# A two-layer transformer block in one program: the first norm of layer 1 with its sums, root and reciprocal on token partitions

## The reference

```python
def rmsnorm(x, g):
    xf = x.astype(jnp.float32)
    y = xf * lax.rsqrt(jnp.mean(xf * xf, axis=-1, keepdims=True) + EPS)
    return (y * g.astype(jnp.float32)).astype(x.dtype)

hx = rmsnorm(x, norm1_g[i]) * (1 + sc1x) + sh1x
hc = rmsnorm(ctx, norm1_g[i]) * (1 + sc1c) + sh1c
(qn_x, qr_x, kn_x, kr_x, v_x), rest_x = mixer_features(hx, *feat_w, rope)
(qn_c, qr_c, kn_c, kr_c, v_c), rest_c = mixer_features(hc, *feat_w, None)
```

## Time and profile before

| | us |
|---|---|
| three runs | 1464.16, 1463.48, 1463.38 |
| median | 1463.48 |
| span of the profiled execution, first to last instruction | 1461.5 |
| mean granted clock of TensorE in it | 0.998 of full |

### The profile page before, as it was taken

One profiled execution on the slowest core, in us unless ns is written; L12 is line 12 of the kernel. 1 busy time (PEld: TensorE's weight loads), 2 busy tenths in 40 slices (PEclk: granted clock), 3 DMA queues, 4 the chain that ended last, 5 costly groups with the idle time before them and its releaser, 6 DMA issues.

```text
span 1461.5 us, 20681 instructions
## 1 busy us (share of the span) xinstructions
PE 1418.0 (97%) x7952; PEld 1225.0 (84%) x7952; DVE 1003.8 (69%) x1537; ACT 521.3 (36%) x833; POOL 85.7 (6%) x139
## 2 busy tenths in 40 slices
PE   6999899999999999999999999989999999999998
PEld 3788698889888888888888878868998888888887
DVE  5587988778867666656665688788757555555555
ACT  4342866234222122222121225466445233223321
POOL 0023700000000000000000000350000000000000
PEclk9999999999999999999999999999999999999999
DMA  9643011332643243325333411301022322322324
GB/s 386 278 132 99 1 44 61 130 114 101 200 130 115 88 142 115 106 95 155 118 95 106 138 49 58 115 15 44 15 97 92 101 86 100 100 86 86 114 92 139
DMA packets 42983, 158.62 MB, mean 109 GB/s; under 512 B 5168, under 2 KB 6576, under 8 KB 41776
## 3 DMA queue, kind: packets, MB, share of 16 engines
q1 hardware_dynamic: 42928, 157.87, 32.3%
HBM read 155.76 MB, written 2.10 MB: 108 GB/s over the span
## 4 chain that ended last, share of the span: by engine, by line
PE 84%; DVE 9%; ACT 3%; DMA 2%; issue 1%; SPq 0%; DVEq 0%; ACTq 0%
PE ps L708 67%; PE ps L646 4%; PE ps L647 4%; PE ps L648 4%; DMA ada_step<-in_w_step 1%; DVE w_lo L1373 1%; DVE tmp L1473 1%; PE ps L858 1%; PE ps L660 1%; DVE H_lo L1482 1%; DMA w_raw<-in_w_main 1%; DVE nmax L1687 1%; DVE qn L1660 1%; DVE pt_lo L1488 1%; DVE part_sums L1635 1%
## 5 line engine op out<-in xcount | busy, mean ns | idle before, releaser
L708 PE MATMUL ps<-H_hi,w_hi 128*128 128x512 f32 (+1 forms) x1280 | 449.1, 351 | 4.2 <-DVE H_lo L1482 1.7
L708 PE MATMUL ps<-H_lo,w_hi 128*128 128x512 f32 (+1 forms) x1280 | 447.4, 350 | 0.0
L708 PE MATMUL ps<-H_hi,w_lo 128*128 128x512 f32 (+1 forms) x1280 | 447.1, 349 | 0.0
L1045 ACT ACTIVATE w_hi<-w_raw 128x1024 fp32r<-128x1024 f32 x180 | 187.5, 1055 | 423.3 <-PE ps L708 368.3
L708 PEld LDWEIGHTS ps<-H_hi,w_hi 128*128 128x128 f32 x1280 | 242.3, 189 | 38.3 <-DVE H_lo L1482 3.2
L708 PEld LDWEIGHTS ps<-H_hi,w_lo 128*128 128x128 f32 x1280 | 242.2, 189 | 31.6
L708 PEld LDWEIGHTS ps<-H_lo,w_hi 128*128 128x128 f32 x1280 | 242.3, 189 | 30.8
L1495 DVE SCALAR_TENSOR_TENSOR X<-ps,mod,X 128x512 f32<-128x512 f32 (+1 forms) x296 | 180.8, 644 | 108.5 <-PE ps L708 87.3
L1373 DVE TENSOR_TENSOR w_lo<-w_raw,w_hi 128x1024 fp32r<-128x1024 f32 x180 | 221.1, 1239 | 37.5 <-ACT w_hi L1045 36.4
L708 PE MATMUL ps<-inner_hi,w_hi 128*128 128x512 f32 (+1 forms) x528 | 187.6, 355 | 0.3 <-DVE X L1495 0.3
L708 PE MATMUL ps<-inner_lo,w_hi 128*128 128x512 f32 (+1 forms) x528 | 187.2, 355 | 0.0
(11 more groups left out here) (200 smaller groups left out, 1846.8 us busy)
## 6 DMA issues: line engine op xcount, KB each, us to landing
w_raw<-in_w_main SPq DMA_DIRECT2D x182, 512.0 KB, 3.3
ada_raw<-in_w_ada SPq DMA_DIRECT2D x73, 512.0 KB, 4.1
ada_step<-in_w_step SPq DMA_DIRECT2D x7, 2048.0 KB, 14.6
X<-in_x SPq DMA_DIRECT2D x2, 1024.0 KB, 6.8
cb<-in_cvec SPq DMA_DIRECT2D x2, 1024.0 KB, 7.3
out_x<-X SPq DMA_DIRECT2D x8, 256.0 KB, 4.6
rtab<-in_rope SPq DMA_DIRECT2D x4, 384.0 KB, 7.2
X<-in_ctx SPq DMA_DIRECT2D x2, 512.0 KB, 7.9
```

The costliest lines, as they stand in the source:

```text
L708: ins = pe.matmul(job.ps(a, b), ww[:, wsl], xx[:, xk, a:b], start=first and n == 0, stop=last and n == 2)
L1045: act.activation(w_hi[c % 4][:], w_raw[c % 2][:], ACT.Copy).then_inc(chunk_hi, 1)
```

## The change

The first norm of layer 1 takes the form of the second norms, with differences.

- **x sums.** The eighth x square isn't added on DVE. PE makes `x_rows` at the place of the old sum: for each of 4 token tiles `ss` and `tmp[1]` (the last square) as stationary operands against two columns of ones. ACT takes the root of 4 columns (`layer_root`), DVE the reciprocal and two halves of `diag` (`layer_inverse`), PE spreads tokens 0 to 255 ahead of the seventh ctx product and tokens 256 to 511 ahead of the eighth (`x_spread`), ACT copies each to `ss` (`x_spread_out`). The slot is freed by the second copy.
- **ctx sums.** The eight ctx squares aren't added on DVE. PE sums each with two matmuls for two token tiles (`ctx_rows`), two squares in each of pieces 1, 3, 4 and 5, after the second token tile of the piece. A square's buffer is free when PE has summed it. ACT takes the root after `high` of piece 6, DVE the reciprocal and `diag` after `low` of piece 6, PE spreads ahead of piece 8, ACT copies after `high` of piece 8, and DVE's `scaled` of piece 9 waits for that copy.
- **The table of the root** is loaded ahead of the x squares of layer 0's end instead of behind them.
- No DMA is added, removed or moved.

```diff
...
-    SUM_AT = 6
+    CTX_SQUARES_AT, CTX_ROOT_AT, CTX_INVERSE_AT, CTX_SPREAD_AT, CTX_OUT_AT = (1, 3, 4, 5), 6, 7, 8, 8
+    LAYER_INVERSES, LAYER_SPREADS, LAYER_DIAGS = (0, 2), (0, 1), (0, 3)
...
-        def norm_sum_job(nn, n):
-            job, (_, a, b) = Job(JOB["sum", nn][n]), nsegs(nn)[n]
+        def norm_sum_job(n):
+            job, (_, a, b) = Job(JOB["sum", 0][n]), nsegs(0)[n]
-            pe.wait_ge(ss_done[nn], 2 + (len(DVE_SQUARES) if nn == 0 else (KD, 2 * KD)[n]))
-            job.filled(pe.matmul(job.ps(a, b), ones[:], ss[:, a:b], start=nn > 0, stop=True))
+            pe.wait_ge(ss_done[0], 2 + len(DVE_SQUARES))
+            job.filled(pe.matmul(job.ps(a, b), ones[:], ss[:, a:b], start=False, stop=True))
+        def x_rows():
+            job = Job(JOB["sum", 2][0])
+            job.open(pe)
+            pe.wait_ge(ss_done[2], 2 + KD - 1)
+            pe.wait_ge(sq_done[2], KD)
+            for t in range(XTOK):
+                out, tsl = job.ps(NX + 2 * t, NX + 2 * t + 2), slice(P * t, P * (t + 1))
+                pe.matmul(out, ss[:, tsl], ones[:, 0:2], start=True, stop=False)
+                last = pe.matmul(out, tmp[(KD - 1) % 2][:, tsl], ones[:, 0:2], start=False, stop=True)
+            last.then_inc(ss_done[2], 1)
+        def x_spread(part):
+            job = Job(JOB["sum", 2][0])
+            pe.wait_ge(diag_done[1], part + 1)
+            o = (NX + 2 * P) * part
+            ins = pe.matmul(job.ps(o, o + 2 * P), ones[:], diag[:, 2 * part:2 * part + 2], start=True, stop=True)
+            if part:
+                job.filled(ins)
+            else:
+                ins.then_inc(spread_done[1], 1)
+        def ctx_rows(m):
+            job = Job(JOB["sum", 2][1])
+            if m == 0:
+                job.open(pe)
+            pe.wait_ge(sq_done[2], KD + m + 1)
+            for t in range(XTOK, TOK):
+                o = NX * (t - XTOK)
+                last = pe.matmul(job.ps(o, o + 2), tmp[m % 2][:, P * t:P * (t + 1)], ones[:, 0:2],
+                                 start=m == 0, stop=m == KD - 1)
+            last.then_inc(ss_done[2], 1)
+        def ctx_spread():
+            job = Job(JOB["sum", 2][1])
+            pe.wait_ge(diag_done[1], 3)
+            job.filled(pe.matmul(job.ps(0, NC), ones[:], diag[:, 0:NC // P], start=True, stop=True))
...
-            pe.wait_ge(diag_done[nn // 2], n + 1)
+            pe.wait_ge(diag_done[nn // 2], LAYER_DIAGS[nn // 2] + n + 1)
...
-            norm_sum_job(0, n)
+            norm_sum_job(n)
-                if L == 1 and n == SUM_AT:
-                    norm_sum_job(2, 1)
+                if L == 1 and n == CTX_SPREAD_AT:
+                    ctx_spread()
...
+                    if L == 1 and t == ta // P + 1 and n in CTX_SQUARES_AT:
+                        for m in range(2):
+                            ctx_rows(2 * CTX_SQUARES_AT.index(n) + m)
...
-                        norm_sum_job(2, 0)
+                        x_rows()
+                    if s == 1 and m in (6, 7):
+                        x_spread(m - 6)
...
-        def root_job(nn, n):
-            job, (_, a, b) = Job(JOB["sum", nn][n]), nsegs(nn)[n]
+        def root_job(n):
+            job, (_, a, b) = Job(JOB["sum", 0][n]), nsegs(0)[n]
+        def layer_root(n):
+            job, nt = Job(JOB["sum", 2][n]), (XTOK, TOK - XTOK)[n]
+            act.wait_ge(ss_done[2], (1, 2)[n] * KD + 2)
+            if n == 0:
+                src = job.ps(NX, NX + 2 * nt).rearrange("p (t s) -> p s t", s=2)[:, 0]
+            else:
+                src = job.ps().rearrange("p (t s) -> p s t", s=NX)[:, 0]
+            act.activation(tok_rms[:, 4 * n:4 * n + nt], src, ACT.Sqrt, bias=vec[:, V_EPS:V_EPS + 1],
+                           scale=1.0 / D).then_inc(root_done[2], 1)
+        def x_spread_out(part):
+            job, o = Job(JOB["sum", 2][0]), (NX + 2 * P) * part
+            if part:
+                job.ready(act)
+            else:
+                act.wait_ge(spread_done[1], 1)
+            ins = act.activation(ss[:, 2 * P * part:2 * P * (part + 1)], job.ps(o, o + 2 * P), ACT.Copy)
+            if part:
+                job.last_read(ins)
+            else:
+                ins.then_inc(rms_ok[2], 1)
+        def ctx_spread_out():
+            job = Job(JOB["sum", 2][1])
+            job.ready(act)
+            job.last_read(act.activation(ss[:, NX:NT], job.ps(0, NC), ACT.Copy))
...
-            act.wait_ge(spread_done[nn // 2], n + 1)
+            act.wait_ge(spread_done[nn // 2], LAYER_SPREADS[nn // 2] + n + 1)
...
-            root_job(0, n)
+            root_job(n)
...
-                root_table()
-                root_job(2, 0)
+                layer_root(0)
+                for part in range(2):
+                    x_spread_out(part)
-                    if n in (1, 3, 4, 5):
-                        for m in range(2 * (n - 1 - (n > 1)), 2 * (n - (n > 1))):
+                    if n in CTX_SQUARES_AT:
+                        for m in range(2 * CTX_SQUARES_AT.index(n), 2 * CTX_SQUARES_AT.index(n) + 2):
-                    if n == 7:
-                        root_job(2, 1)
+                    if n == CTX_ROOT_AT:
+                        layer_root(1)
+                    if n == CTX_OUT_AT:
+                        ctx_spread_out()
...
+                root_table()
...
-                dve.wait_ge(spread_done[nn // 2], n)
-            dve.wait_ge(tok_inv[nn // 2], n + 1)
+                dve.wait_ge(spread_done[nn // 2], LAYER_SPREADS[nn // 2] + n)
+            dve.wait_ge(tok_inv[nn // 2], LAYER_INVERSES[nn // 2] + n + 1)
+        def layer_inverse(n):
+            x = tok_rms[:, 0:XTOK] if n == 0 else tok_rms[:, 4:4 + TOK - XTOK]
+            dve.wait_ge(root_done[2], n + 1)
+            dve.reciprocal(x, x).then_inc(tok_inv[1], 1)
+            dve.wait_ge(tok_inv[1], n + 1)
+            for part in range(2 - n):
+                if n:
+                    dve.wait_ge(spread_done[1], 1)
+                dve.tensor_tensor(diag[:, 2 * part:2 * part + 2], ident[:].unsqueeze(1).to_broadcast([P, 2, P]),
+                                  x[:, 2 * part:2 * part + 2].unsqueeze(2).to_broadcast([P, 2, P]),
+                                  ALU.mult).then_inc(diag_done[1], 1)
...
-            elif kk == 0:
+            elif kk == 0 and nn == 0:
...
-            if kk < 2 and nn % 2 == 0:
+            if nn == 2 and n == 0:
+                dve.wait_ge(rms_ok[2], 1)
+            elif nn == 2 and kk == 0:
+                Job(JOB["sum", 2][n >= half(2)]).taken(dve)
+            if kk < 2 and nn == 0:
...
-                scaled(2, 0)
+                layer_inverse(0)
+                scaled(2, 0)
...
-                    if n < 7:
-                        for m in range(2 * (n - 3), 2 * (n - 2)):
-                            add_squares(2, KD + m, NX, NT)
+                    if n == CTX_INVERSE_AT:
+                        layer_inverse(1)
...
-                add_squares(2, KD - 1, 0, NX)
```

## The result

The changed kernel takes **1466.94 us**, median of 15 runs (1465.85 to 1468.95), against 1463.48 (15 runs, 1462.69 to 1466.31) before: +3.46 us, ratio 1.0024 [1.0017, 1.0031]. The profiled execution took 1466.38, with a span of 1464.6 and a mean clock of 0.999. The forecast was 1466.6.

What follows compares the result with a forecast made beforehand. DVE bounds the early pieces, PE pieces 4 to 8, the ctx chain the stage's end. +0.2 at piece 0, −1.5 at piece 1, −0.3 before piece 8, then +3.1 to the end: 1463.48 + 3.1 = 1466.6 us; range 1464.6 to 1468.4.

Steps and rivals of the forecast that it cites:

- Start of the sums: Layer 1's first norm: with one DVE add gone (0.70 us), PE can start the x sums at 870.65 instead of 871.37.
- `x_rows`: PE's x sums: sixteen instructions at 0.1125 us take 1.8 us, ending at 872.5 like the old sum; earlier start eaten up.
- the disputed term: Price of two-column matmuls on PE: 0.1125 us each, so 3.6 us for 32 `ctx_rows` instructions; bounds −1.7 to +7.4.
- Rival F: Two-column matmuls cost nothing, their work lying under the neighbours': −1.7, 1461.8 us; chance 0.01.
- Forecast A: The main forecast: late ctx spread shifts the stage's end by +3.1, giving 1466.6 ±0.7 us; chance 0.66.
- Rival B: PE's clock falls as well, near 881 to 885 us: +1.5 more, 1468.1 us; chance 0.12.
- The spread of ctx: Ahead of piece 8: first ctx piece scaled at 899.95 against 896.84, 3.1 us late; PE idle 1.8 us.
- Rival C: The ctx spread is early enough, so piece 8 doesn't wait behind it: −0.9, 1462.6 us; chance 0.10.
- Behind it: After the ctx spread: ctx pieces, splits, loads and copy start 3.1 us later; PE waits 1 us for chunk 4, reaching 916.7.
- In full to the end: From the scaling of ctx onward, the +3.1 us shift lasts to the end; PE is full from 914 to 957.
- The table load: ACT's 1.28 us load of the root's table moves to its wait for the first x update: hidden, costs nothing.
- Rival D: The square lacks a place in the root's table, so another 1.28 us load precedes the x squares: +4.4, 1467.9 us; chance 0.06.

Runs made afterwards that it cites:

- the wide sums: The changed kernel with 128 columns of ones instead of two in `x_rows`, same sums: 1465.76 us, +2.44 against the kernel before, ratio 1.0016.
- the ctx part alone: Only the ctx sums changed against the kernel before, with x summed, rooted and inverted as before: 1471.43 us, +8.11, ratio 1.0057.
- spread at 7: The changed kernel with the ctx spread on PE ahead of piece 7 instead of piece 8: 1464.56 us, +1.24 against the kernel before.
- x part alone: Only the x sums changed against the kernel before, with ctx squares added on DVE again: 1462.93 us, −0.39, ratio 0.9999.
- `latr` first: The changed kernel with DVE's first layer-1 copy to `latr` ahead of the low part of chunk 6: 1465.94 us, +2.39 against the kernel before.
- the mended change: The changed kernel with ctx spread ahead of piece 7, 128-column x sums and x spreads one product earlier: 1463.33 us, −0.15 against the kernel before.
- the earlier x spreads: The x-part kernel with 128-column sums, plus both x spreads one ctx product earlier and `high` of piece 0 before the second copy: 1461.06 us, against 1461.31 without.

## Why the prediction was right

**Start of the sums.** `x_rows` at 869.76, 870.58 on before's clock; forecast 870.65. Right.

**`x_rows`.** Sixteen instructions in 1.91 us, forecast 1.8; the fall touches the last of them. The price of 0.1125 each, which was the disputed term, held: eight `ctx_rows` instructions begin at 881.33, and the second instruction of the stream behind them at 882.43, 1.10 us later, as it was at 44.82, and piece 1 to the ctx spread lasts 19.77 us against the forecast 15.8 + 3.6 + 0.1. Rival F falls. The Trainium skill (TensorE: Matmul & The Clock Gate, section "Back-to-back issue gap") would have 25 ns each. Here every two-column matmul brings its own stationary operand, and at most the first two of a row start so close (0.03 us); the others follow at 0.11.

**The clock, the step that failed.** The forecast had PE at full speed between 872 and 876 us: 0.12 for a product's matmul, the first spread at 873.9, piece 0 at 877.1, piece 1 at 879.4. Measured, on before's clock: 875.20, 878.62 and 880.81. The missing 1.4 us are the clock at half: with the wide sums, and so without the fall, the first spread and piece 1 are at 873.91 and 879.28. The 1.5 us of gain at piece 1 was gone with it. Forecast A had put the clock's part at nothing. Rival B had a fall, at the old place at 881 and for the old reason, PE's standing still; the place and the cause were wrong, and that its price (+1.5) came out is luck, as it was worked out for other instructions. The Trainium skill (same page, section "HAM oscillation — how this bites in real kernels") has waits between bursts bring the array to half rate. The fall of before at 881, and that of the ctx part alone, fit this, though the waits in the Trainium skill's example are of 3 to 5 us and these are of 1.51 and 2.52. The one at 871.4 does not fit: PE is busy for 5.00 of 5.00 us around it, and for 5.01 of the 5.40 us ahead of it (866 to 871.4). Two-column sums had it in four of four profiles (the change, spread at 7, x part alone, `latr` first), 128-column sums in none of five. The mean clocks of all timed executions agree: none of 48 with two-column sums reaches 1.000, five of 55 with wide ones do.

**The spread of ctx.** Spread to scaled piece 1.05 us, forecast 1.05; PE idle for 1.66 ahead of piece 8, forecast 1.8; DVE's 4.90 of waiting for ACT's copy as foretold. Rival C falls: the lead was nil. The earlier spread confirmed it with 2.2 us.

**Behind it.** PE waited 0.74 for the low part of chunk 4 (forecast 1), and the wait for `latr` was still there. Ahead of the second `a2` product all is 4.74 us later on before's clock: the forecast 3.1, the 1.4 of the head, and 0.3 by which piece 1 to the spread took longer than forecast. "In full to the end" was not quite so. Near 1100 us a wait for `w_lo`, 1.19 before, is 0.85 now and takes up 0.3. At the very end, from the end of DVE's last update to the end of the span, it is 3.4 us in before's profile and 2.8 in this one, another 0.6. And the medians differ by less than the traces do up to the second `a2` product in every kernel with the ctx sums on PE: 3.46 against 4.74 here, 1.24 against 2.22 with the earlier spread, 2.44 against 3.17 with wide sums, 8.11 against 8.90 for the ctx part alone, so by 0.7 to 1.3 us. The two places make 0.9 of it here. Whether the 0.6 at the end belongs to the kernels or to the two executions, one profile of each cannot tell, for executions of one kernel differ by as much: of the 75 of the kernel before that were timed beside the experiments, the 12 with the mean clock of its profile (0.998) took 1462.72 us in the median, the 63 with a lower one 1463.55. So 1466.6 fell close to 1466.94 partly by luck: something overlooked (1.6 up to the second `a2` product) and something neglected (1.3 behind it) nearly cancel.

**The table load.** At 857.28, one, hidden where ACT waits 1.52 us for the first x update. Rival D falls.

**The verdict by mechanism.** Work moved from DVE, which PE last waited for at piece 4, to PE, which had no slack from there on; plus one ordered list that puts a broadcast right before the piece that needs it. Both were in the forecast, and both were shown by runs: the spread moved alone (2.2 us), and the mended change against the same kernel with the ctx sums on DVE (2.3 us).

## What to carry to other kernels

Before work is moved off an engine, ask in which stretch it is late: here DVE was late above all for pieces 0 and 1 (1.51 and 2.52 us, then 0.18 at piece 4), so the x half of the change pays (−2.2 to −2.7 us with wide sums) and the ctx half, which burdens PE where it is full, cost 2.3 us even in the best form tried. A result that makes a round over PE, ACT and DVE needs its step on PE well ahead of the consumer in PE's list; one piece, 2.4 us, did it here. Before a step is moved forward in one list, look at what it pushes back in the others: the earlier x spreads won nothing for that reason. And tiny matmuls are not cheap: they took 0.11 us each, and a row of sixteen brought the clock down for what followed.

## What was not expected of the hardware

- Sixteen float32 instructions with 128×128 stationary and two moving columns, back to back, were followed by a granted clock of 0.50 for 3.4 us (6.8 in one profile), though PE had stood still for only 0.4 of the 5.4 us before. The same sums with 128 columns kept it at 1.00 and lasted no longer themselves, 1.81 us against 1.91. That the width is what counts is shown by the exchange; why is not. Eight in a row, as in `ctx_rows`, four times between 881 and 894 us, left the clock at 1.00.
- After idle times of 1.51 and 2.52 us the clock stood at half for 3.4 us in the kernel before and for 10.2 in the ctx part alone. PE's list differs by `ctx_rows` alone, but the longer fall began 1.7 us earlier, at 879.5, and the first `ctx_rows` only at 883.1, so they are not its start. What makes the difference the runs don't show.
- Falls of the clock come and go from one execution to the next where no kernel has an edit. Of the eleven profiles five have one between 22 and 28 us; against before's, which has it, DVE in that of the change gains 1.1 us there. Six have one between 981 and 994 us. A comparison of two single profiles has to be made from a common instruction near the stage.
- Two halves of a change cost 7.7 us when measured apart and 3.5 together, since one of them removes the idle time on which the other's worst cost hangs.
